# One decoder layer: a third seven-product group in the down product, and the last pair's tiles ahead of the last unit

## The reference, cut to what matters

```
x = x + 0.5 * swiglu(rms_norm(x, g_ffn1), w1, w3, w2)       # stage 0: 1024 -> 2816 -> 1024
z = rms_norm(x, g_mix) @ w_in + b_in                         # mixer: 14 column tiles of 128
x = x + concat(attention(q, k, v), gated mlp(u, v)) @ w_out + b_out
x = x + 0.5 * swiglu(rms_norm(x, g_ffn2), w1, w3, w2)       # stage 1
gate = sigmoid(rms_norm(x, g_ple) @ w_ple_gate); x = x + gate * (p @ w_ple_proj)
```

## Time and profile before

| | |
|---|---|
| median of 3 runs | 945.49 us |
| the profiled execution | 945.73 us |
| its span, first to last instruction | 944.2 us |
| busy: TensorE, VectorE, ScalarE, GpSimd | 930.5, 699.5, 553.1, 257.7 us |
| mean granted TensorE clock | 0.998 of 2.4 GHz |
| matmuls | 7750 |

### The profile page before, as it was taken

The page is one execution under the profiler, slowest core; times in us unless marked ns, Lnnn a source line. Parts: engine busy times, 40 slices in busy tenths (PEclk is TensorE's granted clock), DMA queues, the critical chain, the costliest instruction groups (busy, mean ns, idle before and its releaser), DMA issues.

```text
span 944.2 us, 19452 instructions
## 1 busy us (share of the span) xinstructions
PE 930.5 (99%) x7750; PEld 919.5 (97%) x7750; DVE 699.5 (74%) x1164; ACT 553.1 (59%) x893; POOL 257.7 (27%) x190
## 2 busy tenths in 40 slices
PE   7999999999999999999999999999999999999997
PEld 7999999999999999889999999999999999999997
DVE  6979887888777463657975388997788877745586
ACT  7748756667556443665545466766567656635243
POOL 0212222222322046210228412222222222205521
PEclk9999999999999999999999999999999999999999
DMA  8958787778886636312124696887878886753302
GB/s 248 179 102 175 142 178 155 147 165 156 152 170 119 157 90 179 74 46 68 46 78 136 112 179 143 155 172 147 156 159 155 160 171 139 131 151 89 112 24 91
DMA packets 245269, 127.62 MB, mean 135 GB/s; under 512 B 14906, under 2 KB 242580, under 8 KB 245164
## 3 DMA queue, kind: packets, MB, share of 16 engines
q1 hardware_dynamic: 176868, 90.27, 34.4%
q0 software_dynamic: 64272, 31.99, 27.5%
q10 hardware_dynamic: 4040, 4.12, 1.4%
HBM read 123.81 MB, written 3.59 MB: 135 GB/s over the span
## 4 chain that ended last, share of the span: by engine, by line
PE 92%; DVE 4%; ACT 2%; DMA 1%; issue 1%; SPq 0%; ACTq 0%; DVEq 0%
PE ps L2011 56%; PE ps L1918 24%; PE ps L2041 7%; PE ps L2357 2%; PE ps L1952 1%; DMA x_rows<-in_x_prompt_dram 1%; DVE w_lo L1616 1%; PE ps L2259 1%; PE ps L2230 0%; DVE tt L1634 0%; SPq L733 0%; DVE tt L1627 0%; DVE probs L1659 0%; ACT tt L1031 0%; PE ps L2381 0%
## 5 line engine op out<-in xcount | busy, mean ns | idle before, releaser
L2011 PE MATMUL ps<-xo_hi,w_lo 128*128 128x260 f32 x1008 | 284.8, 283 | 0.0
L2011 PE MATMUL ps<-xo_hi,w_hi 128*128 128x260 f32 x1008 | 284.4, 282 | 0.0
L2011 PE MATMUL ps<-xo_lo,w_hi 128*128 128x260 f32 x864 | 244.3, 283 | 0.0
L2011 PEld LDWEIGHTS ps<-xo_hi,w_hi 128*128 128x128 f32 x1008 | 189.9, 188 | 0.1
L2011 PEld LDWEIGHTS ps<-xo_hi,w_lo 128*128 128x128 f32 x1008 | 189.9, 188 | 0.0
L1434 DVE TENSOR_TENSOR w_lo<-w_raw,w_hi 128x512 fp32r<-128x512 f32 x156 | 160.6, 1042 | 14.2 <-ACT w_hi L871 6.7
L2011 PEld LDWEIGHTS ps<-xo_lo,w_hi 128*128 128x128 f32 x864 | 162.7, 188 | 0.0
L1207 POOL DMA_DIRECT2D w_lo<-in_w_ffn_dram x52 | 66.8, 1285 | 270.4 <-ACT w_lo L878 270.4
L2011 PE MATMUL ps<-hop_hi,w_lo 128*128 128x260 f32 x448 | 126.7, 283 | 0.0
L2011 PE MATMUL ps<-hop_hi,w_hi 128*128 128x260 f32 x448 | 126.7, 283 | 0.0
L2011 PE MATMUL ps<-hop_lo,w_hi 128*128 128x260 f32 x448 | 126.5, 282 | 0.0
(11 more groups left out here) (310 smaller groups left out, 2181.5 us busy)
## 6 DMA issues: line engine op xcount, KB each, us to landing
w_raw<-in_w_ffn_dram SPq DMA_DIRECT2D x104, 256.0 KB, 4.4
w_lo<-in_w_ffn_dram POOLq DMA_DIRECT2D x104, 256.0 KB, 5.4
w_a<-in_w_ffn_dram SPq DMA_DIRECT2D x36, 512.0 KB, 5.9
w_raw<-in_w_ffn_dram SPq DMA_DIRECT2D x16, 512.0 KB, 5.5
w_a<-in_w_ffn_dram SPq DMA_DIRECT2D x32, 256.0 KB, 4.0
w_raw<-in_w_ffn_dram SPq DMA_DIRECT2D x16, 384.0 KB, 4.7
w_raw<-in_w_in_dram SPq DMA_DIRECT2D x10, 512.0 KB, 4.0
w_lo<-in_w_ffn_dram POOLq DMA_DIRECT2D x9, 512.0 KB, 8.6
```

What stands on the lines that cost most here:

```text
L2011: ins = pe.matmul(ps[:, b, 0:Q], w[:, cc, k * P:(k + 1) * P], m_, start=(first and k == 0 and t == 0), stop=(k == kn - 1 and t == 2), skip ...
```

## The change

- `DN_CHUNKS` has three groups: pairs 0 to 3, 4 to 6, 7 to 9. In the groups of three pairs a product is 9 matmuls, and weight blocks are 384 columns wide. A stage has 30 units (before 26). Only pair 10 is computed in the standard way, 2 k-tiles, 12 matmuls a tile.
- Units 28 and 29 of a stage are the third group's last two. Pair 10's tiles 0 to 5 are issued between them, tile 6 and tile 7 around product 4 of unit 29. The preparation of unit 29's weights is spread over tiles 0 to 5. Its transfers, and those of pair 10's weights (two loads of 512 KB), use cells of the same order of release.
- The high part of x and its square are separate steps; the squares use two buffers, `sq` and `diag`. Each addition into `ssq` waits for the one before it. `ssq` is cleared after the last `dn_b` of the stage, which is in unit 29.
- The low parts of the next weights stay on GpSimd, at new places in the order: behind squares 2, 5 and 7.
- The two p tiles (stage 1) are turned at once before unit 29. `stat_sum` of stage 0 is before k-step 3 of the second mixer tile. The order of the slots of the following weights is changed.

```diff
-MIX_SLOTS = (0, 1, 2, 3)
-LAST_SLOTS = (0, 1, 2, 3, 4, 5)
+MIX_SLOTS = (3, 0, 2, 1)
+LAST_SLOTS = (5, 3, 0, 2, 1, 4)
...
-LAST_DOWN_BANKS = ((6, 1), (0, 1), (2, 3), (6, 1), (0, 1), (2, 1), (0, 1), (2, 1))
-DN_CHUNKS = ((0, 1, 2, 3), (4, 5, 6, 7))
-LAST_PAIRS = (8, 9, 10)
+LAST_DOWN_BANKS = (6, 3, 1, 6, 3, 1, 6, 4)
+P_BANK = (6, 0)
+DN_CHUNKS = ((0, 1, 2, 3), (4, 5, 6), (7, 8, 9))
+LAST_PAIR = 10
...
-            UNITS += tuple(("dn", chunk_, i) for i in range(KD // 2))
+            UNITS += tuple(("dn", chunk_, i) for i in range(KD // 2 - 2 * (pair_ == LAST_PAIR)))
     UNITS += (("up", pair_, 1),)
+UNITS += tuple(("dn", len(DN_CHUNKS) - 1, i) for i in (2, 3))
...
-            if loads[l + 1][0] == "unit":
+            if n < N_UNIT - 2:
                 q = [ahead[0:1], ahead[1:3], ahead[3:6], ahead[6:8], ahead[8:11]]
-            else:
+            elif n == N_UNIT - 2:
                 q = [[], [], [("hi", "last", 0)], [("lo", "last", 0)], [("hi", "last", 1)]]
                 put(n, "f", ("lo", "last", 1))
+            else:
+                q = [[("p_take", 0), ("p_take", 1), ("x_hi", 4)], [("x_lo", 0), ("x_lo", 1)], [("x_hi", 5), ("x_lo", 2)],
+                     [("x_lo", 3)], [("hi", "next", 0), ("sq", 0)]]
+                put(n, "f", ("sq", 1), ("sq", 2), ("x_lo", 4), ("lo", "next", 0))
...
+            if n == N_UNIT - 1:
+                steps += [("sq", 3), ("down", 6), ("comb", n), ("prod", n, 4), ("x_add", 6), *finish(n), ("x_hi", 6)]
+                steps += [("x_lo", 5), ("hi", "next", 1), ("sq", 4), ("x_lo", 6), ("down", 7), ("x_add", 7), ("sq", 5)]
+                steps += [("x_hi", 7), ("lo", "next", 1), ("p_split",), ("x_lo", 7), ("p_split_lo",), ("sq", 6)]
+                steps += [("sq", 7), ("hi", "next", 2), ("lo", "next", 2)]
         else:
-            n, p = N_UNIT - 1, KF // 2 - 1
-            steps += [("down_a", 0), ("comb", n), ("prod", n, 4)]
-            steps += [("down_a", 1), ("h", p), ("h_hi", p), ("hi", "last", 2), ("down_a", 2), ("h_lo", p)]
...
+            n = N_UNIT - 2
+            part = [ahead[0:2], ahead[2:4], ahead[4:7], ahead[7:8], ahead[8:9], ahead[9:11]]
+            for m in range(6):
+                steps.append(("down", m))
+                if m == 0:
+                    steps += [("comb", n), ("prod", n, 4)]
+                steps += part[m] + [("x_add", m)]
+                if m == 0:
+                    steps += finish(n)
+                elif m > 1:
+                    steps.append(("x_hi", m - 2))
+            steps.append(("p_turn",))
...
-        (1, 2): [("stat_sum",)],
+        (1, 3): [("stat_sum",)],
...
+            def square(stat, m, bufs):
+
+                act.wait_ge(x_ready, 8 * stat + m - 7)
+                act.wait_ge(sq_added, max(9 * stat + m - 7 - len(bufs), 9 * stat - 8))
+                nc.scalar.activation(bufs[m % len(bufs)][:], x[:, m, :], ACT.Square).then_inc(sq_made, 1)
...
-            def add_square(stat, m):
-                pool.wait_ge(sq_added, 9 * stat - 8)
+            def add_square(stat, m, buf=sq):
+                pool.wait_ge(sq_added, 9 * stat + m - 8)
                 pool.wait_ge(sq_made, 8 * stat + m - 7)
-                nc.gpsimd.tensor_tensor(ssq[:], ssq[:], sq[:], ALU.add).then_inc(sq_added, 1)
+                nc.gpsimd.tensor_tensor(ssq[:], ssq[:], buf[:], ALU.add).then_inc(sq_added, 1)
...
-                    elif kind == "x_add":
-                        if arg[0] == 0:
-                            pool.wait_ge(combined, N_UNIT * (s + 1))
+                    elif kind == "sq":
+                        m, = arg
+                        if m == 0:
+                            pool.wait_ge(kept_added, N_ADDED * (s + 1))
                             clear_ssq(2 * s + 1)
-                        add_square(2 * s + 1, *arg)
+                        add_square(2 * s + 1, m, (sq, diag)[m % 2])
...
+            def down(s, m):
+                key = ("last", s, m // 4)
+                lo_wait(pe, key)
+                if m == 0:
+                    pe.wait_ge(ab_ready, 4 * s + 4)
+                    pe.wait_ge(h_lo_ready, 11 * (s + 1))
+                elif m == 1:
+                    pe.wait_ge(h_ready, 13 * s + 13)
+                elif m == 2:
+                    pe.wait_ge(combined, N_UNIT * (s + 1) - 1)
+                elif m < 6:
+                    pe.wait_ge(x_ready, 16 * s + m - 2)
+                elif m == 6 and s:
+                    pe.wait_ge(p_ready, 2)
+                elif m == 6:
+                    pe.wait_ge(x_ready, 4)
+                else:
+                    pe.wait_ge(combined, N_UNIT * (s + 1))
```

More of the change, by code:

```diff
@@ L103, in ffn_loads @@
     loads = [("up", (0, 1, 2)), ("up", (3, 4, 5)), ("up", (6, 7)), ("unit", 0)]
-    loads += [("unit", n) for n in range(1, N_UNIT)]
-    return loads + [("last",)]
+    loads += [("unit", n) for n in range(1, N_UNIT - 1)]
+    return loads + [("last",), ("unit", N_UNIT - 1)]
 def ffn_steps():
@@ L165, in ffn_steps @@
     for l, (kind, *arg) in enumerate(loads):
-        ahead = prep(l + 1) if kind != "last" and loads[l + 1][0] != "last" else []
+        ahead = prep(l + 1) if l + 1 < len(loads) and loads[l + 1][0] != "last" else []
         if kind == "up":
@@ L196, in ffn_steps @@
             steps += at.get((n, "f"), []) + [("prod", n, 7)]
-        else:
-            n, p = N_UNIT - 1, KF // 2 - 1
-            steps += [("down_a", 0), ("comb", n), ("prod", n, 4)]
-            steps += [("down_a", 1), ("h", p), ("h_hi", p), ("hi", "last", 2), ("down_a", 2), ("h_lo", p)]
-            between = {0: [("lo", "last", 2)], 2: [("hi", "last", 3)], 3: [("lo", "last", 3)], 5: [("lo", "next", 0)]}
-            behind = {4: [("hi", "next", 0), ("p_turn", 0)], 5: [("hi", "next", 1), ("p_turn", 1)],
-                      6: [("lo", "next", 1), ("p_split",), ("hi", "next", 2)], 7: [("p_split_lo",), ("lo", "next", 2)]}
-            for m in range(KD):
-                steps += [("down_b" if m < 3 else "down", m), ("x_add", m)]
-                steps += between.get(m, []) + [("x_lo", m)] + behind.get(m, [])
+            if n == N_UNIT - 1:
[3 more added lines that the diff above has]
+                steps += [("sq", 7), ("hi", "next", 2), ("lo", "next", 2)]
+        else:
+            n = N_UNIT - 2
[10 more added lines that the diff above has]
+            steps.append(("p_turn",))
     return steps
@@ L226, in weight_plan @@
                 key = ("prod", s, *arg)
-            elif kind in ("down", "down_b"):
+            elif kind == "down":
                 key = ("down", s, arg[0])
@@ L264, in weight_plan @@
             elif kind == "last":
-                for j, ms in enumerate(LAST_LOADS):
+                for j, c in enumerate(LAST_CELL):
                     key = ("last", s, j)
-                    there = half if j < 2 else 1 - half
-                    c, n = 7 * there + LAST_CELL[j], len(ms) * LAST_K // 4
-                    lane = 3 * there + 2 * (j % 2)
-                    slot[key], cell[key] = lane, c
-                    free[key] = max(used[c:c + n])
-                    used[c:c + n] = [done[("down", s, ms[-1])]] * n
-                    arrived[lane] += 16 * len(ms)
-                    raw[key] = arrived[lane]
+                    c += 7 * half
+                    slot[key], cell[key] = SLOT_CELL.index(c), c
+                    free[key] = max(used[c:c + 2])
+                    used[c:c + 2] = [done[("down", s, 4 * j + 3)]] * 2
+                    arrived[slot[key]] += 16
+                    raw[key] = arrived[slot[key]]
                     index[key] = len(index)
@@ L1114, in _ @@
                 x_hi(2, m)
+                square(2, m, (sq,))
             act.wait_ge(out_done, 16 * 8)
@@ L1952, in turn @@
                 return pe.transpose(dst, src, ident[0:n, 0:n])
-            def turn_tile(rows_, s_rows, c, p):
-                for b in range(NB):
-                    turn(ps[:, 2 * p, b * P:(b + 1) * P], rows_[:, b, c * P:(c + 1) * P])
-                return turn(ps[:, 2 * p + 1, 0:TS], s_rows[0:TS, c * P:(c + 1) * P], TS)
             def product(s, n, r):
@@ L2044, in down @@
-                if part != 0:
-                    ins.then_inc(unit_done, 1)
+                                            m_[:, H_SLOT[LAST_PAIR], row, :], start=(k == 0 and n == 0),
+                                            stop=(k == 1 and n == 2))
+                ins.then_inc(unit_done, 1)
             def first_stat_out():
```

94 lines of the change are left out of this document (36 added, 58 removed).

## The result

The changed kernel takes 956.45 us (median of 4 runs, 955.22 to 957.36), the kernel before 945.43 us in the same session (4 runs, 945.30 to 945.51). The ratio is 1.0116, 95% interval 1.0098 to 1.0133: slower by 11 us, where 953.7 was predicted. The profiled execution took 955.22 us, span 953.5.

What follows compares the result with a forecast made beforehand. TensorE's matmul count was taken as the bound in both FFN stages, other engines having been early. -5.8 + 2.0 + 5.2 + 6.1 + 0.3 + 0.4 = +8.2 us on 945.49 gave 953.7, range 948.5 to 959.5 (forecast case 950.5 to 957.5).

Steps and rivals of the forecast that it cites:

- Removed: Down product of both FFN stages: 24 fewer matmuls per stage, 48 in all, at 0.120 us each, -5.8 us.
- Cover in the three-pair units: Shorter units: loads and VectorE's work just fit; small waits where a three-pair unit prepares a four-pair one, +0.3 us.
- A: Turn into pair 10's tiles: after tile 0 TensorE waits for VectorE's unit 28 combination, 1.0 us per stage, +2.0.
- B in stage 0: After unit 29: GpSimd's additions and low parts behind the clear delay the squares' transposes from 18.4 to 23.6, +5.2 us.
- The wait of 0.4 ahead of product 4: Unit 29, stage 0: VectorE's low part of x 4 delays the combination, making product 4 0.4 us late.
- B in stage 1: After unit 29: GpSimd's low parts done at 14.3 and 22.3, the second wanted at 16.2, +6.1 us.
- Rival 3: More is lost: three-pair units wait for loads, or the clock falls in stage 1's gap; 957.5 to 961 us, chance 0.10.
- The signs: Wrong if no TensorE gap there, gaps inside units 15 to 28, or gaps but VectorE's low parts at 0.76 us.
- rival 2: GpSimd is late, but blocking is little or A finds cover: +1 to +5, 946.5 to 950.5 us, chance 0.17.
- ScalarE's queue: Stage 0: mixer loads issued behind the last square delay the copy for the third mixer tile, 0.4 us, bounds 0 to 1.5.
- The root: Computed behind stage 0's squares' transposes, with 0.72 us less cover; costs between 0 and 0.7 us, taken as 0.
- the rule weighed in the prediction: VectorE ops with two SBUF inputs and SBUF-reading GpSimd ops alternate by whole instructions; GpSimd would lose 0.76, trace shows 0.46.

Runs made afterwards that it cites:

- experiment 1: Changed kernel with VectorE's low part of pair 10's second load moved behind tile 1, nothing else changed; 953.44 us, 1.0087 of the kernel before.
- kernel 7: Changed kernel with square additions and next weights' low parts on VectorE, squares summed early in `diag`, pair 10's low part behind tile 1; 947.66 us.
- 8: As kernel 7, but the low part of pair 10's second load again ahead of unit 28's combination; 949.88 us, 1.0046 of the kernel before.
- kernel 10: Changed kernel with added matmuls filling TensorE's gaps ahead of the next weights, 15 and 9 in stage 0, 26 in stage 1; 956.03 us.
- 5: Changed kernel with squares summed in `diag`; GpSimd's squares 0 to 3 and first low part precede unit 29's kept additions; 957.63 us.
- 6: As 5, with VectorE's low part of pair 10's second load also behind tile 1; 956.72 us, 1.0118 of the kernel before.
- 3: Changed kernel with GpSimd's sixteen FFN square additions cut to 64 of 520 columns, leaving out part of the sum; 943.79 us.
- 2: Changed kernel with the next weights' three low parts made by VectorE instead of GpSimd, which keeps clear and additions; 951.00 us.
- kernel 4: Changed kernel with 26 matmuls added in stage 1 ahead of the wait for the first gate weight; 956.12 us, 1.0114 of the kernel before.
- kernel 9: Kernel 7 with ScalarE's mixer transfers split and issued earlier, third square addition behind unit 29's combination; 944.01 us, 0.9982 of the kernel before.

## Why the prediction came out as it did

- **Removed, -5.8.** 48 matmuls fewer, 0.120 us each in the units after. Right.
- **Cover in the three-pair units, 0.3.** It was 0: one piece of 2253 matmuls at 0.120.
- **A, 2.0.** 2.2. Taking away the low part named in the working took the wait away (experiment 1), and the pair 7 and 8 gives 2.2.
- **B in stage 0, 5.2.** 4.9: the transposes came at 23.3 and not 23.6, and TensorE could start on the second weight at 20.8, as counted. The wait of 0.4 ahead of product 4 and that for the first low part are in the profile where the count had them.
- **B in stage 1, 6.1.** 6.7. GpSimd's part is 6.0: the two low parts were done 14.3 and 22.2 after unit 29's first matmul, where the count had 14.3 and 22.3. The second took 3.40 instead of 2.40, as the low part of p met it, and the addition ahead of it 1.85, as a low part of x met that. Of the other 0.7 about 0.6 is the clock. Rival 3 said that it could fall in this gap, for 1 to 3 us. It did, and the gate tile took 2.7 more, but 2.0 of them stood in the wait for the second low part. The rival had priced the matmuls and not asked what waits behind them.
- **The signs.** One of those for "wrong" came up in part: gaps in stage 1 with VectorE's low parts of x 5 to 7 at 0.75 to 1.09, not 1.3 to 2.9. Only stage 0 had them longer (3.69 for two). The meetings cost GpSimd what was counted (1.85 instead of 1.30), and its lateness is what TensorE waited for; that they also cost VectorE time shows as a wait of TensorE in one place, the 0.4 ahead of product 4. And rival 2's own terms add up to +1.1 to +2.5, not to +5; its range reached further than its reasons.
- **ScalarE's queue, 0.4.** 1.1, the term furthest off in its own size. Two things were late, and they ended within 0.05 us of each other. The queue: the last square was made at 18.4 as counted, but the issues took 10.7 us instead of 10.0 and the copy ended at 374.89. The root: VectorE's 128x4 op at 369.84 stood beside GpSimd's third low part and took 1.48 us instead of 0.17, so that the root was spread from 374.13 to 374.93; the prediction named 0 to 0.7 for it and took 0. The third tile began at 374.94. Either alone would have cost nearly all of it: in kernel 10 the root was in time (0.62 us for that op), and TensorE waited 0.42 for the copy.
- **The sum** is right to 1.3 us for the profiled execution (+8.2 forecast, +9.5 measured, +9.1 by the rows), and 2.8 low against the median, because the changed kernel's runs spread over 2.1 us above the profiled one and those of before over 0.2. The prediction assumed that the spread stays; what makes it is not known. That the median still lies in the forecast's 950.5 to 957.5 owes something to misses that cancel: +0.6 for the clock, +0.7 at the third mixer tile and +0.2 for A against -0.3 each for the cover and for B in stage 0.

The trace also bears on the rule weighed in the prediction. In the run with early sums an addition takes 1.59 to 1.61 us on average beside VectorE's ops, and 1.30 alone: GpSimd loses about 0.3 to 0.5 a meeting, VectorE a whole GpSimd op. The Trainium skill's page "SBUF — State Buffer" (section "SBUF: two separate sides") has whichever op comes second wait for the whole instruction of the other engine; on VectorE's side the trace agrees (1.48 us for a low part, a wait of up to one addition), on GpSimd's it shows less than VectorE's 0.75.

One reading behind the prediction held only in part. It said that nearly everything stands behind one point, the clear. With the point moved ahead the waits of B went, but the loss stayed, inside unit 29 (5 and 6). What is shown is this: the waits of B are GpSimd's chain behind the clear, and go when its additions are thin (3), although VectorE is held as much as before; its chain can't be started earlier for nothing, because it then holds ops of VectorE that TensorE needs at once (5 and 6); with the additions and low parts off GpSimd both go (7). Meetings as such are no loss: the kernel before had them at the same mean (1020 ns) and no wait. How much of B in the changed kernel is the meetings and how much the length of the chain no run separates; the prediction's own bounds without blocking (3.2 and 3.1 of 4.9 and 6.0) and the lengthened rows give the meetings a third to a half, which is an estimate.

## What to carry to other kernels

A second engine that is idle for 70% of the span is not free capacity when its ops share SBUF with a busy first one: price a move by the ops that will meet, each costing VectorE up to one GpSimd op, and try the work on VectorE, where it may cost half. A gap of TensorE costs what the chain behind it makes of it: the same half clock cost 0.6 of its 2.7 us where the next wait was late anyway, and by count all of its 1.5 us where nothing was. When a wait is removed, look up what each queue has behind it: kernels 2, 5 and 7 each took away waits of B and were then held by something that had stood in their shadow.

## What was not expected of the hardware

- A VectorE op of 4 columns with one SBUF operand (`var<-rs_t`) took 1.48 us beside GpSimd's low part and clears, 0.62 beside clears alone (kernel 10), and 0.17 without them. The reductions just ahead of it, from PSUM, were not held (0.69 and 0.28).
- GpSimd's clear of 520 columns shows as 1.03 to 1.05 us in kernels 5 to 9, and as 0.53 elsewhere. This is no meeting with VectorE: in each case the row begins inside that of a transfer that GpSimd issues, 0.78 us behind its start, and ends 0.5 us behind its end (kernel 5: the transfer from 343.52 to 344.80, the clear to 345.35), whatever VectorE does.
- A TensorE gap of about 2.2 us left the granted clock at 1.00 in the changed kernel and in kernel 4 (stage 0). It brought it to 0.51 in kernel 1 (357.3 to 360.3), and to 0.62 on average over 4.5 us in kernel 7.
- Spread of the runs: 0.2 to 3.3 us for the kernel before (by session), 2.1 for the changed one, 2.1 with the clock full throughout, 2.8 in kernel 9, where GpSimd has no additions or low parts behind the units (4 to 16 runs each, so the ranges compare only roughly). Neither the clock nor the meetings alone explain it.
